# Expert weights in 2 MB transfers of four neighbouring rows per partition, in a two-layer MoE block and decoder kernel

## The reference, cut to what matters

```python
def ec_moe(h, w_router, w_gate, w_up, w_down):       # h [1, 256, 1024], 16 experts
    cap = 2 * n // 16                                # 32 tokens per expert
    aff = softmax(h @ w_router)
    g, idx = top_k(aff.swapaxes(1, 2), cap)
    xs = h[idx]                                      # [16, 32, 1024]
    a = silu(xs @ w_gate) * (xs @ w_up)              # weights [16, 1024, 1024] each
    y = (a @ w_down) * g
    return zeros.at[idx].add(y)

for l in range(2):
    sh_m, sc_m, g_m, sh_f, sc_f, g_f = split(silu(c) @ ada_w[l] + ada_b[l], 6)
    h = rmsnorm(x, norm_mix[l]) * (1 + sc_m) + sh_m
    x = x + g_m * (differential attention if l == 0 else gated short convolution)(h)
    x = x + g_f * ec_moe(rmsnorm(x, norm_ffn[l]) * (1 + sc_f) + sh_f, ...)
# then a second block: mLSTM and latent attention, cross attention, a feed-forward of 4096
```

## Time and profile before

| | us |
|---|---|
| median of 3 runs | 1836.31 |
| the runs | 1836.31, 1835.78, 1843.34 |
| the profiled execution | 1837.48 |
| its span | 1835.3 |
| PE busy | 1504.0 (82%) |
| DVE busy | 536.1 (29%) |
| ACT busy | 319.9 (17%) |

### The profile page before, as it was taken

The page is one execution under the profiler, slowest core; times in us unless marked ns, Lnnn a source line. Parts: engine busy times, 40 slices in busy tenths (PEclk is TensorE's granted clock), DMA queues, the critical chain, the costliest instruction groups (busy, mean ns, idle before and its releaser), DMA issues. The chain is left out here.

```text
span 1835.3 us, 27299 instructions
## 1 busy us (share of the span) xinstructions
PE 1504.0 (82%) x11332; PEld 1029.8 (56%) x11332; DVE 536.1 (29%) x1085; ACT 319.9 (17%) x564; POOL 26.6 (1%) x52
## 2 busy tenths in 40 slices
PE   4899877887787878788788778787878979779998
PEld 3687455543343434388644434343437757669997
DVE  1135464111110101157411111110111356445554
ACT  3000433000000000053300000000011223244443
POOL 4000100000000000000000000000000000000000
PEclk9999998898878878899888888888889987979999
DMA  9984595799999999975699999999994420335550
GB/s 333 364 295 179 228 345 184 308 420 422 421 422 422 421 422 422 407 256 164 250 370 422 422 422 422 422 422 422 422 400 140 139 72 12 115 106 170 195 173 24
DMA packets 146833, 549.45 MB, mean 299 GB/s; under 512 B 10654, under 2 KB 79248, under 8 KB 97488
## 3 DMA queue, kind: packets, MB, share of 16 engines
q1 hardware_dynamic: 143376, 542.18, 75.3%
q10 hardware_dynamic: 1824, 4.83, 0.7%
q0 software_dynamic: 1568, 1.51, 0.4%
HBM read 547.44 MB, written 1.05 MB: 299 GB/s over the span
## 5 line engine op out<-in xcount | busy, mean ns | idle before, releaser
L663 PE MATMUL bank<-ring,scratch 128*32 128x256 f32 x3968 | 275.6, 446 | 31.8 <-DVE scratch L1238 31.8
L687 PE MATMUL bank<-ring,scratch 128*32 128x512 f32 x1024 | 171.7, 831 | 102.6 <-DMA ring<-in_moe_w_down 99.8
L663 PEld LDWEIGHTS bank<-ring,scratch 128*32 128x32 f32 x3968 | 144.0, 128 | 152.1 <-issue 89.4
L484 PE MATMUL bank<-ring,hT 128*128 128x256 f32 (+1 forms) x832 | 187.6, 386 | 7.1 <-DMA ring<-in_attn_w_in 6.1
L484 PEld LDWEIGHTS bank<-ring,hT 128*128 128x128 f32 x832 | 160.5, 195 | 32.5 <-DMA ring<-in_attn_w_in 6.6
L590 PE MATMUL bank<-scratch_split,ring_split 128*128 128x256 f32 x1344 | 160.0, 280 | 7.0 <-DVE ring_split L1285 2.7
L590 PEld LDWEIGHTS bank<-scratch_split,ring_split 128*128 128x128 f32 x1344 | 158.6, 191 | 9.8 <-issue 4.7
L687 PEld LDWEIGHTS bank<-ring,scratch 128*32 128x32 f32 x1024 | 43.5, 146 | 206.5 <-issue 202.6
L1740 ACT ACTIVATE scratch<-bank 128x256 f32<-128x256 f32 x32 | 12.3, 383 | 833.1 <-PE bank L663 833.1
L697 PE MATMUL bank<-scratch 128*128 128x512 f32 x256 | 117.5, 601 | 31.3 <-DVE scratch L1260 31.3
L652 PEld LDWEIGHTS bank<-scratch,xn 128*128 128x128 f32 x1024 | 131.7, 205 | 16.1 <-issue 14.2
(11 more groups left out here) (363 smaller groups left out, 1221.9 us busy)
## 6 DMA issues: line engine op xcount, KB each, us to landing
ring<-in_moe_w_up SPq DMA_DIRECT2D x128, 1024.0 KB, 21.8
ring<-in_moe_w_down SPq DMA_DIRECT2D x128, 1024.0 KB, 18.6
ring<-in_moe_w_gate SPq DMA_DIRECT2D x120, 1024.0 KB, 16.2
ring<-in_ada_w SPq DMA_DIRECT2D x48, 1024.0 KB, 10.5
ring<-in_w_ff SPq DMA_DIRECT2D x32, 1024.0 KB, 5.2
ring<-in_conv_w_in SPq DMA_DIRECT2D x12, 1024.0 KB, 11.9
ring<-in_attn_w_in SPq DMA_DIRECT2D x10, 1024.0 KB, 13.8
ring<-in_w_in SPq DMA_DIRECT2D x7, 1024.0 KB, 11.9
```

Source lines behind the costliest of these rows:

```text
L484: mm = nc.tensor.matmul(T[:, t * 256:t * 256 + width], lhs[:, k, t * P:(t + 1) * P], W[:, k, :], start=(k == ks[0]), stop=(k == ks[-1]))
L663: mm = nc.tensor.matmul(GU[32 * j:32 * j + 32, m * 256:(m + 1) * 256], xs[:, k, :], W[:, (k % 2) * D + j * 256:(k % 2) * D + (j + 1) * 256 ...
L687: mm = nc.tensor.matmul(Y[n][32 * j:32 * j + 32, :], actT[:, b, 32 * j:32 * j + 32], down[j][0][:, b * D + n * 512:b * D + (n + 1) * 512], ...
```

## The change

The expert weights are loaded two units at a time, in one transfer of 2 MB. Partition p of a transfer takes four neighbouring rows (4p to 4p + 3 of 512), one run of 16 KB, into two adjoining slots: rows 4p and 4p + 1 in the even slot, the others in the odd one. One semaphore stands for a pair, that of the even slot. SP's waits are those for the later unit of a pair. Of the spare places, the first two lie side by side and take one transfer of 2 MB; the other two are apart and take a transfer each, with runs of 8 KB, both under one semaphore.

```diff
 def load_expert(e, s):
-    rows = mats[s // 4][e, (s % 4) * 256:(s % 4 + 1) * 256, :]
-    dst, there_sem, _ = expert_unit(l, e, s)
-    sp.dma_start(dst, rows.rearrange("(p a) n -> p (a n)", a=2)).then_inc(there_sem, 16)
+    rows = mats[s // 4][e, (s % 4) * 256:(s % 4 + 2) * 256, :]
+    rows = rows.rearrange("(p a) n -> p (a n)", a=4)
+    there_sem = expert_unit(l, e, s)[1]
+    if e == 1 and s == 0:
+        sp.dma_start(carve(S, 0, 2 * UNIT), rows).then_inc(there_sem, 16)
+    elif e == 1 and s == 2:
+        for h in range(2):
+            sp.dma_start(extra[2 + h], rows[:, h * UNIT:(h + 1) * UNIT]).then_inc(there_sem, 16)
+    else:
+        sp.dma_start(pair_tile(l, e, s), rows).then_inc(there_sem, 16)
...
-left = (("ao11", "ao11", "o0T.2", "lgp0"), ("conv_b.3", "out1.3", "out1.3", "lgp1"))[l]
-for s in range(4):
-    product(sp, left[s])
+for s in (0, 2):
+    product(sp, ("o0T.2", "out1.3")[l] if s == 0 else f"lgp{l}")
     load_expert(1, s)
-for s in range(4, SLOTS):
-    sp.wait_ge(MOE_READ, 12 * e0 + s - 3)
+for s in range(4, SLOTS, 2):
+    sp.wait_ge(MOE_READ, 12 * e0 + s - 2)
     load_expert(1, s)
...
 with sp.Fori(3, NEXP) as e:
-    for s in range(SLOTS):
-        sp.wait_ge(MOE_READ, e * 12 + (12 * (e0 - 1) + s + 1))
+    for s in range(0, SLOTS, 2):
+        sp.wait_ge(MOE_READ, e * 12 + (12 * (e0 - 1) + s + 2))
         load_expert(e, s)
```

The order of the contraction follows. The gather and the router's transposes now pick every fourth column as stationary operand, the gate and up products read two of every four neighbouring columns as moving operand, and so do the ada products of the two chunks (3 and 4) that make the shift and scale of the second modulation:

```diff
 def pair_cols(k):
-    return slice(256 * (k // 2) + k % 2, 256 * (k // 2) + 256, 2)
+    return slice(512 * (k // 4) + k % 4, 512 * (k // 4) + 512, 4)
+def expert_cols(W, j):
+    return W[:, 512 * (j // 2):512 * (j // 2) + 512].rearrange("q (p h b) -> q p h b", h=2, b=2)[:, :, j % 2, :]
...
-    GU[32 * j:32 * j + 32, m * 256:(m + 1) * 256], xs[:, k, :],
-    W[:, (k % 2) * D + j * 256:(k % 2) * D + (j + 1) * 256],
+    GU[32 * j:32 * j + 32, m * 256:(m + 1) * 256].rearrange("q (p b) -> q p b", b=2),
+    xs[:, k, :], expert_cols(W[:, (k % 2) * D:(k % 2) * D + D], j),
```

```diff
 def ada(l, c):
-    empty(v, f"ada{l}.{c}", V.tensor_tensor(row, T..., row, ALU.add))
+    if c == 0:
+        empty(v, f"ada{l}.{c}", V.tensor_tensor(row, T, row, ALU.add))
+    else:
+        V.tensor_copy(row[:, 2 - c, :], T[:, 2 - c, :])
+        q = c - 1
+        empty(v, f"ada{l}.{c}", V.tensor_tensor(row[:, q, :], T[:, q, :], row[:, q, :], ALU.add))
```

More of the change, by code:

```diff
@@ L325, in build @@
         landed = [sem(f"landed{s}") for s in range(SLOTS)]
-        extra_landed = [sem(f"extra_landed{i}") for i in range(len(extra))]
+        extra_landed = [sem(f"extra_landed{i}") for i in range(2)]
         unit_read = sem("unit_read")
@@ L730, in _ @@
                     pe_turn_rows_after(pe, "nx")
-            pe.wait_ge(loads["rows"], 16 * (len(ROWS) + 1))
+            pe.wait_ge(loads["rows"], 16 * (len(ROWS) + 3))
             T = tile(pe, "vec")
             nc.tensor.transpose(T[:, 0:NROWS], vec_rows[0:NROWS, :], ident[0:NROWS, 0:NROWS])
-            for a in range(2):
-                mm = nc.tensor.transpose(T[:, P + 8 * a:P + 8 * a + 8], ffn_rows[:, a::2], ident[0:8, 0:8])
+            for a in range(4):
+                mm = nc.tensor.transpose(T[:, P + 12 * a:P + 12 * a + 12], ffn_rows[:, a::4], ident[0:12, 0:12])
             done("vec", mm)
@@ L1140, in ada @@
                 T = product(v, f"ada{l}.{c}")
-                row = ada_rows[l][c]
-                empty(v, f"ada{l}.{c}", V.tensor_tensor(row, T[:, :].rearrange("p (a n) -> p a n", a=2), row, ALU.add))
+                row, T = ada_rows[l][c], T[:, :].rearrange("p (a n) -> p a n", a=2)
+                if c == 0:
[4 more added lines that the diff above has]
+                    empty(v, f"ada{l}.{c}", V.tensor_tensor(row[:, q, :], T[:, q, :], row[:, q, :], ALU.add))
             def ada_cols(l, n):
@@ L1990, in _ @@
                 g.dma_start(vec_rows[at:at + n, :], a).then_inc(loads["rows"], 16)
-            g.dma_start(ffn_rows, w["norm_ffn"].rearrange("l (u q) -> (l u) q", q=SEQ)).then_inc(loads["rows"], 16)
+            g.dma_start(ffn_rows[0:4, :], w["norm_ffn"].rearrange("l (v q) -> (l v) q", q=512)).then_inc(loads["rows"], 16)
+            for l in range(2):
+                g.dma_start(ffn_rows[4 + 4 * l:8 + 4 * l, :],
+                            w["ada_b"][l].rearrange("(r q) -> r q", q=512)[6:10, :]).then_inc(loads["rows"], 16)
             g.wait_ge(landed[7], 16)
@@ L2001, in _ @@
             for l in range(2):
-                for a in range(2):
-                    small.append((router[:, l, a::2, 0:NEXP],
-                                  w["router_w"][l].rearrange("(u p a) e -> a p u e", p=P, a=2)[a]))
+                for a in range(4):
+                    small.append((router[:, l, a::4, 0:NEXP],
+                                  w["router_w"][l].rearrange("(v p a) e -> a p v e", p=P, a=4)[a]))
             small.append((gate_bias[:, 0:1], w["b_igate_2"].rearrange("a h -> h a")))
@@ L2097 @@
 TWO_PI = _two_pi()
-N_SMALL = 16
+N_SMALL = 20
 AHEAD = 3
```

53 lines of the change are left out of this document (34 added, 19 removed).

## The result

The changed kernel takes 1844.94 us (median of 20 runs, 1838.63 to 1850.72), the kernel before in the same session 1837.43. The ratio is 1.0035, with a 95% interval of 1.0023 to 1.0046. Timed once more later it was 1842.83 us and 1.0024 (1.0011 to 1.0038). The forecast of 1826 missed in size and in sign. The profiled execution took 1839.4 us (span 1837.3), a low one among its runs: its span is only 2.0 us over that of the earlier trace rows, and that of a second profile of the same kernel is 1847.0. More than half of the distance lies behind the mixtures. From the combine of the last expert (its products at L710) to the first product of the final feed-forward the first profile has 275.5 us and the second 281.1, and the granted clock differs there.

What follows compares the result with a forecast made beforehand. The weights' arrival was taken to bound the expert loops. Longer runs -13.2 us, pairs' delay +2.2 and small edits +0.4 gave -10.6, and so a forecast of 1826 us, range 1820 to 1842.

Steps and rivals of the forecast that it cites:

- What bounds the kernel; the worth of a run: Expert loops: weights' arrival sets the end; each run costs 9.4 ns, so 16 KB runs give 428 GB/s, up from 422.
- The rival that a long run costs as much per byte: Weight transfers: a 16 KB run costs as two, giving little or no gain; 1839 or 1834 us, chance 0.25.
- What this saves, and what the pairs delay: Expert loops: longer runs save 13.2 us in both layers, waiting for pairs at the start costs 2.2.
- The delay term: Loop start: first load waits for two units, 1.7 us later; net +1.1 us per layer, +2.2 in both.
- What PE's reads cost: Gather at step 4 and gate and up's moving operand at two of four: taken as costing nothing.
- The cover of the steady part: Expert loops: PE has 5.7 us to spare per expert, 29.83 against 24.1, covering a slower warm gather.
- The slow rival: Gather and router's transposes: strided reads take twice as long, make PE late, break the stream once; 1861 us, chance 0.12.
- The argument on rates: Gather: step 2 is free, and step 4's cold 16-byte pieces pass at step 2's warm rate; no cost.
- The small edits: Kernel start and bias steps: more row and router loads, two transposes, split bias additions; +0.4 us, bounds 0 to 1.

Runs made afterwards that it cites:

- e3: Changed kernel with 1 MB transfers (8 KB runs, waits of before) and the input written so the gather reads neighbours: 1845.75 us, 1.0040 against the kernel before.
- e1: Changed kernel with the normalised input written in the weights' row order, so gather and router read neighbouring columns: 1838.78 us, 1.0007 against the kernel before.
- e16: Changed kernel with 1 MB transfers, neighbouring columns of an unpermuted input and old addresses, only its time used: 1839.40 us, 1.0012 against the kernel before.
- e17: Changed kernel, 2 MB transfers kept, with neighbouring columns of an unpermuted input and old addresses, only its time used: 1832.04 us, 0.9968 against the kernel before.
- e13: e6 with the first load of the expert loop split into two 1 MB transfers, the first after one unit is read: 1831.11 us, 0.9970 against the kernel before.
- e6: e1 with ffn_vec moved behind the scratch and 64 unused bytes in its old place, other tensors as before: 1832.75 us, 0.9975 against the kernel before.
- e5: Kernel before with one unused tensor of 128 bytes per partition behind ffn_gain, moving later addresses only: 1842.08 us, 1.0014 against the kernel before.
- e10: Changed kernel with ffn_vec moved behind the scratch and 64 unused bytes in its old place, gather step kept: 1839.88 us, 1.0014 against the kernel before.
- e18: Changed kernel timed once more, nothing altered, in the session of e16 and e17: 1842.83 us, 1.0024 against the kernel before.
- e4: Kernel before with its gather taking every fourth column instead of every second, only its time used: 1844.56 us, 1.0037 against the kernel before.

## Why the prediction was wrong, by its steps

**What bounds the kernel; the worth of a run.** Right. 2411 ns plus 4 runs of 9.4 ns were to give 428 GB/s, and the windows have 428 and 429; the period between down products in e1 is 29.4 us, as forecast. The rival that a long run costs as much per byte is out; whether the halved number of transfers has a share in it wasn't separated. The Trainium skill's "DMA: Bandwidth & Descriptors", section "Why small descriptors are slow (HBM only)", holds joining descriptors in one packet worth while at 256 B or less. Transfers with runs of 16 KB in place of 8 KB are worth 7 to 8 us here (e3 to e1, e16 to e17), and the measurement decides.

**What this saves, and what the pairs delay.** The sum was -13.2 + 2.2 = -11 us. Without the gather's step the layers gain 9.3 to 9.6 us (e17, e1). The delay term had its parts right (first load 1.7 us later) and its consequence wrong, at least in the first layer: e13 takes the delay away and that layer stays as it is. So the term is 0 there instead of +1.1, in the second layer between 0 and that, and the saving nearer to 9.5 than to 13.2 us. Up to about 400 us PE's reads hold the stream back, however fast it is: from 331 to 401 e6 moved 28.0 MB, e13 28.1 and the kernel before, which is 1.0 us ahead of e6 at its first gather and has the slower rate, 28.4. A faster stream earned nothing there.

**What PE's reads cost: the step that failed.** It read "warm the cover is 5.7 us per expert". The gather's growth, 3.6 us, is indeed less than the 5.7, and in the steady part it is covered. At the loop's start it isn't. Two paragraphs earlier the same text had found the stream's tightest margin to be 1 us at 381.5, where SP waits for PE's reads. Two warm gathers make those reads 7.2 us late, and waiting for two units adds 1.7 (392.76 against 379.83, of which 3.9 were there when PE began the first expert's products). The queue runs dry, and the stream, which bounds everything after, never makes up for it: 6.7 us in the first layer's windows. The cover of the steady part was applied to the two experts that don't have it. The slow rival had this mechanism and its place. It also had its 6.7 us, in part by luck: it took one break where the windows have two, and the first layer of the changed kernel is 5.1 us longer than e1's in one profile and 6.3 in the other. It got a chance of 0.12 because the rest of its price, 10.7 us per layer at the low clock, was rightly thought unlikely.

The argument on rates holds by its numbers and was read wrongly. A gather product loads 128 columns, and its pace is the row's time over 32. Step 4 takes one 16-byte piece per column: 7.67 us / 32 / 128 = 1.87 ns per piece at the low clock, 7.45 / 32 / 128 = 1.82 at the high one. Step 2 takes 64 pieces in 3.84 / 32 = 120 ns: 1.88 ns per piece. Neighbouring columns take 3.65 / 32 = 114 ns. So step 2 was no proof of free strides. The three paces fit a limit of about 1.85 ns per piece, at which step 2 just sat, and where one more doubling doubles the time; that the piece is of 16 bytes is the forecast's premise, and these paces alone don't show it. At the low clock a product takes 7.03 / 32 = 220 ns at step 2 already, so step 4 adds only 20 to it, and the router's transposes stay at 3.66 / 16 = 229. The Trainium skill's "SBUF — State Buffer", section "Door 1: The DMA port swizzle", says that SBUF needs at least two hits on a 16-byte line for full bandwidth. The traces agree: with two hits 120 ns, with one 233. The same note gives a stride of 4 fp32 as free; for the gather's step of 4 the measured 233 ns say otherwise, and the measurement decides.

The moving operand at two of four was to be free; 64 products of gate and up take 3.83 us at the high clock (366.17 in the changed kernel's timeline) for 3.64 (359.04 in that of before), 5% more. In e1, which has this and not the gather's step, the stream doesn't break.

**The small edits.** Forecast +0.4 (0 to 1), measured about 3 (e16, e17), with an interval of e16 that takes in the forecast. And one edit had no term at all: the tensor that grew by 128 bytes. It costs 2 to 6 us in totals (e5 over before 2.6; changed to e10 2 to 4; e1 to e6 6), and 3.4 us in the final feed-forward stage by the profiles' averages.

**The sum with what the runs showed.** The transfers of 2 MB -9.3, gather's step +8 (e1 to the changed kernel) to +12.7 (e17 to e18), 128 bytes +3.4, small edits +3: +5 to +10 us, against +4.4 and +6.4 by the two measured ratios (5.2 and 7.5 by the medians). The upper part of the sum isn't reached. In most pairs of kernels a difference in the layers came out smaller in the total (e4: 10.4 in the layers, 6.8 in total). The layers come from single profiles, and behind them the changed kernel's own two differ by 5.6 us, with a granted clock of 0.94 and 0.79 at 1540 to 1600, so part of it is that spread. What else is in it stays open.

## What to carry to other kernels

Cover is not one number: where PE's progress releases the buffers for a saturated stream, take each added microsecond against the margin at the loop's first iterations, not against the mean slack of the steady part. A layout that makes transfers longer can change how the operands are read. Permute the small operand once when it is written, rather than step through it at every use (e1 against the changed kernel, 5 us). And after resizing a small tensor look at stages that the edit doesn't touch; padding to the old address is a one-line test (e10, e6).

## What the runs showed of the hardware that I had not expected

- A product with 128 fp32 columns as stationary operand and 32 moving columns (the gather) takes 114 ns with neighbouring columns, 120 with a step of 2 and 233 with a step of 4 at the high clock; at the low one 220 with a step of 2 and 240 with a step of 4.
- Moving all later tensors by 128 bytes goes with fp32r products of 128x512 at a median of 394 or 397 ns in place of 392, in seven profiles against thirteen, and with a final stage 3.4 us longer. In the one profile with 256 bytes it has 392 ns and 180.9 us.
- An ACTIVATE of 128x1024 fp32 takes 1.15 us in order and 2.1 with a step on its input or its output; DVE's TENSOR_SCALAR of the same shape goes from 0.75 to 1.15 us.
- The rates fit 9.4 ns per run up to 16 KB: 348, 387, 422 and 428 GB/s with runs of 1 KB, 2 KB on average, 8 KB and 16 KB, the last in transfers of 2 MB.
- Two executions of one kernel can be granted a different clock in the same stage: 0.94 and 0.79 at 1540 to 1600 in the changed kernel's two profiles, which are 5.6 us apart in the stages around it.
